# Retention stage of a two-block transformer kernel: values centred while they are turned, context states added in PSUM, hand-written order for each engine, and outputs passed on from SBUF

## What is computed

```python
def _ret_final_state(k, v, log_gamma):
    w = jnp.exp(log_gamma.astype(F32)[None, :] * jnp.arange(T - 1, -1, -1, dtype=F32)[:, None])
    return jnp.einsum('bthk,bthv->bhkv', k * w[None, :, :, None], v)
# per chunk, forwards and (flipped) backwards
    scores = jnp.einsum('bhik,bhjk->bhij', qc, kc) * d_intra
    o = jnp.einsum('bhij,bhjv->bhiv', scores, vc) + jnp.einsum('bhik,bhkv->bhiv', qc * q_decay, s)
    s = c_decay * s + jnp.einsum('bhjk,bhjv->bhkv', kc * k_decay, vc)
# in the token mixer
    o_r = _head_layernorm(o_rf + _flip(o_rb), ret_norm_w) * jax.nn.silu(rg)
    out = jnp.concatenate([o_g, o_r], axis=-1) @ w_out
```

## Time and profile before

| | |
|---|---|
| median of 3 runs | 3810.3 us (3804.82 to 3817.7) |
| the profiled execution | 3809.31 us, its span 3807.5 us |
| PE busy, share of the span | 3524.9 us, 93% |
| DVE, ACT, POOL busy | 2190.0, 1529.1, 734.2 us |
| last projection matmul of `in2` starts | 2691.4 us |
| retention stage on PE (to the first `out2` matmul) | 146.47 us, PE busy 89.59, DVE 91.30, ACT 58.35 |
| first output tile of `out2` done | about 2853 us |

### The profile page before, as it was taken

How to read it: one execution, slowest core, us unless ns; L and a number is a source line. 1 busy time by engine, 2 the same in 40 slices (tenths; PEclk the granted TensorE clock), 3 DMA queues, 4 the chain that set the end, 5 groups by cost and what they waited for, 6 DMA issues and landing times.

```text
span 3807.5 us, 45943 instructions
## 1 busy us (share of the span) xinstructions
PE 3524.9 (93%) x18417; PEld 2895.9 (76%) x18417; DVE 2190.0 (58%) x2898; ACT 1529.1 (40%) x1900; POOL 734.2 (19%) x334
## 2 busy tenths in 40 slices
PE   6999999999899899999998789999769699999996
PEld 4566677677687688888886567777547699999996
DVE  3343446545366555545325444545654899999996
ACT  3344442334222221121124433333342677777774
POOL 2111111122123222222223111111011222222210
PEclk9999999999999999999999999999889899999998
DMA  3111113143553144444311113132532899999996
GB/s 126 40 50 56 56 61 123 56 149 125 188 189 127 45 138 142 151 150 149 97 39 49 58 68 135 63 117 92 155 114 80 335 378 378 380 384 382 377 378 244
DMA packets 127268, 611.68 MB, mean 161 GB/s; under 512 B 14353, under 2 KB 15769, under 8 KB 102226
## 3 DMA queue, kind: packets, MB, share of 16 engines
q1 hardware_dynamic: 122306, 591.44, 42.4%
q0 software_dynamic: 4608, 16.78, 1.7%
q10 hardware_dynamic: 144, 0.52, 0.0%
HBM read 525.39 MB, written 83.27 MB: 160 GB/s over the span
## 4 chain that ended last, share of the span: by engine, by line
PE 81%; DVE 9%; ACT 4%; DMA 3%; issue 2%; POOL 1%; SPq 0%; DVEq 0%; ACTq 0%; POOLq 0%
PE bank L264 17%; PE bank L266 17%; PE bank L265 17%; PE bank L3085 4%; PE bank L3087 4%; PE bank L3086 4%; PE bank L3097 2%; PE bank L3095 2%; PE bank L3096 2%; PE bank L616 2%; PE bank L585 1%; PE bank L594 1%; PE bank L605 1%; DVE stg L1619 1%; DVE res L854 1%
## 5 line engine op out<-in xcount | busy, mean ns | idle before, releaser
L264 PE MATMUL bank<-XH,WH 128*128 128x512 f32 (+1 forms) x2696 | 1085.2, 403 | 97.1 <-DVE XL L2018 16.2
L266 PE MATMUL bank<-XH,WL 128*128 128x512 f32 (+1 forms) x2696 | 1055.4, 391 | 0.0
L265 PE MATMUL bank<-XL,WH 128*128 128x512 f32 (+1 forms) x2696 | 1053.5, 391 | 0.0
L252 POOL TENSOR_TENSOR WL<-WR,WH 128x1024 fp32r<-128x1024 f32 (+1 forms) x249 | 494.3, 1985 | 2161.1 <-ACT WH L244 2161.1
L264 PEld LDWEIGHTS bank<-XH,WH 128*128 128x128 f32 x2696 | 512.1, 190 | 267.0 <-issue 76.8
L265 PEld LDWEIGHTS bank<-XL,WH 128*128 128x128 f32 x2696 | 513.5, 190 | 108.8 <-issue 6.3
L266 PEld LDWEIGHTS bank<-XH,WL 128*128 128x128 f32 x2696 | 512.9, 190 | 105.7
L244 ACT ACTIVATE WH<-WR 128x1024 fp32r<-128x1024 f32 (+1 forms) x249 | 216.5, 870 | 612.6 <-PE bank L266 592.0
L3026 DVE TENSOR_TENSOR EL<-ER,EH 128x2816 fp32r<-128x2816 f32 x120 | 369.1, 3082 | 4.0 <-POOL warm L3269 4.0
L3021 ACT ACTIVATE EH<-ER 128x2816 fp32r<-128x2816 f32 x120 | 306.5, 2563 | 151.7 <-PE bank L3087 89.0
L3085 PE MATMUL bank<-EH,WH 128*128 128x352 f32 x1024 | 335.6, 328 | 1.5 <-DVE WL L3187 1.5
(11 more groups left out here) (511 smaller groups left out, 5009.0 us busy)
## 6 DMA issues: line engine op xcount, KB each, us to landing
ER<-in_wu_dram SPq DMA_DIRECT2D x48, 1408.0 KB, 9.1
ER<-in_wd_dram SPq DMA_DIRECT2D x40, 1408.0 KB, 9.6
aq<-in_w_ada_dram SPq DMA_DIRECT2D x96, 512.0 KB, 3.9
WR<-in_w_in_dram SPq DMA_DIRECT2D x89, 512.0 KB, 4.5
ER<-in_wg_dram SPq DMA_DIRECT2D x32, 1408.0 KB, 8.1
res<-in_wg_dram SPq DMA_DIRECT2D x16, 1408.0 KB, 8.5
res<-in_wu_dram SPq DMA_DIRECT2D x16, 1408.0 KB, 8.6
WR<-in_wg_dram SPq DMA_DIRECT2D x16, 1408.0 KB, 8.3
```

The costliest lines, as they stand in the source:

```text
L252: e.tensor_tensor(WL[:, n % 2 * 1024:n % 2 * 1024 + m], raw, hi.bitcast(F32), ALU.subtract).then_inc(*w_lo.up("w_lo", n))
L264: e.matmul(bank[bk][:, 0:b - a], whi, xhi, start=k == 0, stop=False)
L265: e.matmul(bank[bk][:, 0:b - a], whi, xlo, start=False, stop=False)
L266: mm = e.matmul(bank[bk][:, 0:b - a], wlo, xhi, start=False, stop=k == K - 1)
```

## The change

**Values.** The values are no longer turned by a transpose but by a product with a constant matrix, the identity minus 1/128 everywhere (`cn("mneg")`, made by DVE much earlier), which turns and centres them at once. The mean of the output is then zero, so `ret.msum` and `ret.mean` go. ACT squares straight from PSUM, then copies out.

**States.** The key copy of the further context chunk gets one chunk's decay more (`far`), and PE adds the two context chunks in PSUM. Each direction has eight products in two groups of four (`G8`), the second in bank 0 or 1. DVE's recurrence is one copy and seven multiply-adds per direction, written straight into the slots of `Ss`.

**Tables.** Masking and adding of `Dm` is done by POOL (`ret_pool_`), and its scale goes into DVE's multiplication of the scores.

**Order.** `ret_interleave` goes; the calls for each engine are written out. The rotations for head 1 are done inside the stage.

**Handing on.** `h2`, the landing place of the `D_o` tiles, lies over keys and values in `RM`. SP loads tiles 0 to 5 when head 3's scores are formed. Tiles 6 and 7 (heads 2 and 3) aren't stored; `out2` reads them where they are, in `aq`. The small transfers of router weights and `D_m5` come after the last `out2.lo`.

```diff
+    def ret_pe_(e):
+        e.wait_ge(*on("ret.cen"))
+        ret_v_pe(e, 0)
+        ret_k_pe(e, 0)
+        ret_scores_pe(e, 0)
+        ret_v_pe(e, 1)
+        ret_states_pe(e, 0)
+        ret_k_pe(e, 1)
+        ret_states_pe(e, 1)
+        ret_out_pe(e, 0)
+        ret_scores_pe(e, 1)
+        ret_root_pe(e, 0)
+        ret_k_pe(e, 2)
+        ret_v_pe(e, 2)
+        ret_out_pe(e, 1)
+        ret_states_pe(e, 2)
+        ret_scores_pe(e, 2)
+        ret_root_pe(e, 1)
+        ret_v_pe(e, 3)
+        ret_k_pe(e, 3)
+        ret_states_pe(e, 3)
+        ret_scores_pe(e, 3)
+        ret_out_pe(e, 2)
+        ret_root_pe(e, 2)
+        ret_out_pe(e, 3)
+        ret_root_pe(e, 3)
+
+    def ret_v_pe(e, h):
         e.wait_ge(*on("ret.v", h))
+        for c0, n in G10:
+            b = 6 + c0 // 4 % 2
+            e.wait_ge(*on.bank(b, "ret.vT", h, "N", c0))
+            for cc in range(c0, c0 + n):
+                mm = e.matmul(bank[b][:, (cc - c0) * 128:(cc - c0) * 128 + 128],
+                              rmem[h % 2]["v"][:, cc * 128:cc * 128 + 128], cn("mneg"), start=True, stop=True)
+            mm.then_inc(*ret_pe.up("ret.vT", h, "T", c0))
...
+    def ret_states_pe(e, h):
+        M = rmem[h % 2]
+        e.wait_ge(*on("ret.kT", h, "N", 8))
+        e.wait_ge(*on("ret.vT", h, "N", 8))
+        for n0, n in G8:
             for d in range(2):
+                b = d if n0 else 6 + d
+                e.wait_ge(*on.bank(b, "ret.S", h, d, n0))
                 for q in range(n0, n0 + n):
-                    cc = ORDERS[d][q]
...
+                    pair = ORDERS[d][0:2] if q == 0 else ORDERS[d][q + 1:q + 2]
+                    for i, cc in enumerate(pair):
+                        mm = e.matmul(bank[b][:, (q - n0) * 128:(q - n0) * 128 + 128],
+                                      M["keN"][d][:, cc * 128:cc * 128 + 128], M["vN"][:, cc * 128:cc * 128 + 128],
+                                      start=i == 0, stop=i == len(pair) - 1)
+                mm.then_inc(*ret_pe.up("ret.U", h, d, n0))
...
-        for k in range(2):
-            b = B_S[1][k]
-            e.wait_ge(*on("ret.ov", h, k))
-            e.wait_ge(*on.bank(b, "ret.mean", h, k))
-            e.matmul(bank[b][:, :], ones, M["o"][:, half(k)], start=True, stop=True).then_inc(*P.up("ret.msum", h, k))
...
+    def ret_out_act(e, h):
+        M = rmem[h % 2]
         for k in range(2):
             e.wait_ge(*on("ret.o", h, k))
+            e.activation(M["Ss"][1][:, half(k)], bank[B_S[1][k]][:, :], AF.Square).then_inc(*ret_act.up("ret.sq", h))
             if h > 1:
                 e.wait_ge(*on("o", 4 + h - 2))
...
+    def ret_pool_(e):
+        for h in range(4):
+            Dm = rmem[h % 2]["Dm"]
+            for d, mk in enumerate(("mle", "mge")):
+                e.wait_ge(*on("ret.dm", h, d))
+                e.tensor_tensor(Dm[:, d * 128:d * 128 + 128], Dm[:, d * 128:d * 128 + 128], cn(mk), ALU.mult).then_inc(
+                    *ret_pool.up())
+            e.wait_ge(*ret_pool.now)
+            e.tensor_tensor(Dm[:, 0:128], Dm[:, 0:128], Dm[:, 128:256], ALU.add).then_inc(*ret_pool.up("ret.mask", h))
...
+        ret_queries_dve(e, 0)
+        ret_scores_dve(e, 0)
+        ret_rope_dve(e, 1, "k")
+        ret_rope_dve(e, 1, "q")
+        ret_states_dve(e, 0)
+        ret_queries_dve(e, 1)
+        ret_scores_dve(e, 1)
+        ret_states_dve(e, 1)
+        ret_rope_dve(e, 2, "k")
+        ret_rope_dve(e, 2, "q")
+        ret_gate_dve(e, 0)
+        ret_norm_dve(e, 0)
+        ret_rope_dve(e, 3, "k")
+        ret_queries_dve(e, 2)
+        ret_scores_dve(e, 2)
+        ret_states_dve(e, 2)
+        ret_rope_dve(e, 3, "q")
+        ret_gate_dve(e, 1)
+        ret_norm_dve(e, 1)
+        ret_queries_dve(e, 3)
+        ret_scores_dve(e, 3)
+        ret_states_dve(e, 3)
+        ret_gate_dve(e, 2)
+        ret_norm_dve(e, 2)
+        ret_gate_dve(e, 3)
+        ret_norm_dve(e, 3)
...
+        e.wait_ge(*on("ret.sc", 3, 1))
+        for j in range(6):
+            e.wait_ge(*on("o", j))
+            e.dma_start(tj(h2, j), D_o[j]).then_inc(*d_fl[j].up("out2.o", j))
...
-        for s in d_o:
-            e.wait_ge(*s.end)
         for h in range(2):
             for j in range(8):
                 o = j * T + h * 512
-                e.wait_ge(*on("out2.o", h, j))
-                e.activation(XH3[:, o:o + 512], h2[:, o:o + 512], AF.Copy).then_inc(*A.up("out2.hi", h, j))
+                if j < 6:
+                    e.wait_ge(*on("out2.o", j))
+                e.activation(XH3[:, o:o + 512], out2_in(j)[:, half(h)], AF.Copy).then_inc(*A.up("out2.hi", h, j))
```

More of the change, by code:

```diff
@@ L2493, in ret_sp @@
         join(e, "in2")
[L2494 to L2502 removed]
+        ret_load_sp(e, 0, "g")
+        ret_load_sp(e, 1, "g")
+        for h in range(2):
             e.wait_ge(*on("ret.vT", h, "T", 8))
@@ L2581, in ret_act_ @@
     def ret_act_(e):
-        A = ret_act
         join(e, "gla")
         join(e, "in2")
-        ret_interleave([ret_head_act(e, h) for h in range(4)])
-    def ret_head_act(e, h):
-        A, M = ret_act, rmem[h % 2]
-        Dm = M["Dm"]
-        yield
+        ret_tables_act(e, 0)
+        ret_tables_act(e, 1)
+        turn_act(e, ret_act, rmem[0]["vN"], ("ret.vT", 0))
+        ret_k_act(e, 0)
+        turn_act(e, ret_act, rmem[1]["vN"], ("ret.vT", 1))
+        ret_k_act(e, 1)
+        ret_out_act(e, 0)
@@ L2606, in ret_head_act @@
             e.wait_ge(*on("ret.kT", h, "T", c0))
+            b = bank[6 + c0 // 4 % 2]
             for d in range(2):
-                e.activation(M["keN"][d][:, c0 * 128:(c0 + n) * 128], bank[6 + c0 // 4 % 2][:, 0:n * 128], AF.Identity,
-                             scale=lg[:, 16 + 4 * d + h:17 + 4 * d + h]).then_inc(*A.up("ret.kT", h, "N", c0))
-        yield
-        yield
-        yield
-        yield
-        yield
+                near, far = lg[:, 16 + 4 * d + h:17 + 4 * d + h], lg[:, 32 + 4 * d + h:33 + 4 * d + h]
+                if c0 < 8:
+                    e.activation(keN[d][:, c0 * 128:(c0 + n) * 128], b[:, 0:n * 128], AF.Identity, scale=near).then_inc(
+                        *ret_act.up("ret.kT", h, "N", c0))
+                else:
+                    for i in range(2):
+                        e.activation(keN[d][:, (8 + i) * 128:(9 + i) * 128], b[:, i * 128:i * 128 + 128], AF.Identity,
+                                     scale=far if i == d else near).then_inc(*ret_act.up("ret.kT", h, "N", c0))
@@ L2664, in ret_first_dve @@
             st.upto("ret.first", i)
-        for j, (h, x) in enumerate(((0, "k"), (1, "q"), (1, "k"))):
-            ret_rope_dve(e, h, x)
+        ret_rope_dve(e, 0, "k")
+        for j in range(3):
             st.upto("ret.first", 2 + j)
     def ret_dve_(e):
-        V = ret_dve
         join(e, "gla")
@@ L2723, in ret_head_dve @@
                                                ALU.add).then_inc(*V.up("ret.S", h, d, n0))
-                    prev[d] = dst
-        yield
-        yield
-        yield
-        yield
-        for k in range(2):
-            e.wait_ge(*on("ret.msum", h, k))
-            e.scalar_tensor_tensor(o_[:, half(k)], bank[B_S[1][k]][:, :], -1.0 / 128, o_[:, half(k)], ALU.mult,
-                                   ALU.add).then_inc(*V.up("ret.mean", h, k))
-        yield
-        yield
-        yield
+                    prev[d] = to
@@ L2781, in out2_sp @@
         join(e, "ret")
-        for s in d_o:
-            e.wait_ge(*s.end)
-        for h in range(2):
-            for j in range(8):
-                if h:
-                    e.wait_ge(*on("out2.o", 0, j))
-                e.dma_start(tj(h2, j)[:, half(h)], D_o[j][:, half(h)]).then_inc(*d_fl[j].up("out2.o", h, j))
         for j in range(8):
@@ L2815, in out2_pe @@
         e.wait_ge(*on("out2.m5c"))
-        e.wait_ge(*on.bank(0, "out2.m5"))
-        e.transpose(bank[0][0:8, 0:128], cf[:, 0:8], ident).then_inc(*P.up("out2.m5T"))
+        e.wait_ge(*on.bank(7, "out2.m5"))
+        e.transpose(bank[7][0:8, 0:128], cf[:, 0:8], ident).then_inc(*P.up("out2.m5T"))
         for m in range(8):
@@ L2906, in out2_dve @@
         join(e, "ret")
-        for s in d_o:
-            e.wait_ge(*s.end)
         e.scalar_tensor_tensor(cs_[:, 16:24], mod[:, 32:40, 0], 1.0, pr("norm2", 0, 8), ALU.add, ALU.mult).then_inc(*V.up())
         e.tensor_copy(cf[:, 0:8], mod[:, 40:48, 0]).then_inc(*V.up("out2.m5c"))
-        e.wait_ge(*on("out2.m5T"))
-        e.tensor_copy(ac2[0:8, 0:128], bank[0][0:8, 0:128]).then_inc(*V.up("out2.m5"))
         for h in range(2):
@@ L2915, in out2_dve @@
                 out2_lo(e, V, h, j)
+        e.wait_ge(*on("out2.lo", 1, 7))
+        e.wait_ge(*on("out2.m5T"))
+        e.tensor_copy(ac2[0:8, 0:128], bank[7][0:8, 0:128]).then_inc(*V.up("out2.m5"))
         w3 = wr_.rearrange("p (j e) -> p j e", e=16)
@@ L3297, in pe_program @@
         st.rest("in2", "end")
-        ret_interleave([ret_head_pe(e, h) for h in range(4)])
+        ret_pe_(e)
         out2_pe(e)
```

(1 more changed line is left out.)

195 lines of the change are left out of this document (84 added, 111 removed).

## The result

The changed kernel takes 3779.71 us, the median of 7 runs (3769.93 to 3792.79), against 3811.14 us for the kernel before in the same session (7 runs, 3804.82 to 3817.7): a ratio of 0.9917, 95% interval 0.9903 to 0.9931, so about 0.8% faster. The prediction was 3777, range 3763 to 3793. The profiled execution took 3782.39 us.

The account below looks back on a forecast made before the run. Hand-overs between engines were taken to bound the retention stage; 26.8 us less by head 3's end plus 6.0 at the hand-over made 32.8 less, from 3809.3 to 3776.5, said as 3777 us, range 3763 to 3793.

Parts of the forecast that it names:

- The sum: Whole kernel: 26.8 us less up to head 3's end plus 6.0 at the hand-over, 32.8 us less in all.
- What bounds the stage: Retention stage, 146.5 us: no engine is full, hand-overs between engines bound it, and savings should arrive whole at the end.
- States in PSUM: Heads' chunk products: DVE loses one step per direction, 0.8 us a head; PE's 28.0 us of waiting for the recurrence go.
- Centring: Heads' mean: 8.8 us of PE products and 5.3 of DVE subtractions go; turning values costs 1.1 us a head more.
- Tables to POOL: Masks of the heads: DVE loses 16 small operations, about 4.4 us; holding up between POOL and DVE costs 2.
- Written order: DVE's new list in the stage: 74.7 us of work, 32.0 of waits; head 3 ends at 2804, 26.8 us less.
- The walk: Stage's engine lists summed in order with old durations; the old lists came out 2.8 us late, which was taken off.
- Rival 2: Engine lists of the heads: late entries in fixed lists bring two more stalls of 8 us, kernel 3793 us; 14%.
- Handing on: Head 3's end to the first out2 tile: ACT starts sooner, out2.lo limits; 5.4 to 9.8 us less, 6.0 taken.
- The clock: PE in the stage: about a fifth of its work at 1.2 GHz, as the granted clock before was 0.80.
- rival 1: PE in the stage stays at the low clock: 12 to 13 us slower than before, kernel 3822 us; 3%.
- rival 4: PE in the stage does nearly no work at the low clock: kernel 3765 us; 13%.

Follow-up runs that it names:

- c4: The changed kernel with other lists for PE, ACT and DVE, found by a search with a walk over the lists: 3756.6 us, ratio 0.9866.
- c2: The kernel before with only the context states changed (added in PSUM, eight regions a direction, second four in banks 0 and 1): 3786.43 us, ratio 0.9944.
- a3: The changed kernel with PE's list altered, scores of heads 1 to 3 ahead of their chunk products: 3773.97 us, ratio 0.9914.
- a4: a3 with the context states of before, nine regions a direction in banks 6 and 7 only: 3785.93 us, ratio 0.9938.
- b3: The changed kernel with values turned by transposes again and the mean left out of the computation: 3778.42 us, ratio 0.9921.
- c1: The kernel before with the centring alone added, its order, states, masks and hand-over kept: 3804.19 us, ratio 0.9989.
- b1: The changed kernel with the mask products and their sum back on DVE, ahead of each head's scores: 3779.88 us, ratio 0.9922.
- a1: The changed kernel with its new operations called in the interleaved order of before: 3775.83 us, ratio 0.991.
- b4: The changed kernel with the old hand-over, heads 2 and 3 stored and half tiles loaded after all stores: 3786.06 us, ratio 0.9938.

## Why the prediction was right, step by step

**The sum.** It said 32.8 us less. The medians differ by 31.4, the profiled executions by 26.9 (3809.31 and 3782.39). In the profiles head 3 ends 23.8 us earlier instead of 26.8, the hand-over gives 6.6 instead of 6.0, and 3 us are lost behind the stage, which the sum had not. That the median of the changed kernel came within 3 us of 3777 is in part luck: its runs lie 22.9 us apart, and the profiled one is 5.4 us above it.

**What bounds the stage: right, with half of the gain in DVE's work.** Hand-overs bound it: with the same operations, c4 took another 20.7 us out of the stretch by order alone. But of the 24.4 us of the change itself DVE's own work gave 12.0 (88.0 to 76.0 us, the stretch less DVE's idle times in it) and its waits 12.4 (44.5 to 32.1). And what was saved arrived at the end but for 3 us.

**States in PSUM: the step that carries the result, and the prediction named its mechanism.** "PE's 28.0 us of waiting go" came true, and what it named as next, the turn that needs banks 6 and 7, is the 9.2 us of c2. Alone in the old order this part gives 22.8 us (c2), and taken back from a3's lists it costs 17.3 (a4).

**Centring.** A product turns at 1.8 times the cost of a transpose (12.8 against 7.1 us of PE for four heads), close to the factor of two taken from the earlier trace rows. By the Trainium skill's "4× faster for FP32" (TensorE: Matmul & The Clock Gate, Terms), 7.1 would have become 28.4, an estimate; the measurement decides against it. On the path the product costs 0.7 us (b3). Centring as a whole gave 4.9 us in the old order (c1).

**Tables to POOL: the sum had 4.4 of gain and 2 of cost; b1 has nothing.** The cost in longer DVE operations was about right (1.5 us), the gain was not, since the 3.1 us that go from DVE stood ahead of a wait (b1 leaves the scale, the rest of the 4.4, where the change put it). The prediction's estimate by the "exclusive lock" of the Trainium skill's SBUF — State Buffer (SBUF: two separate sides) was also that the move gives nothing. That agrees with b1, but not for its reason: the cost is 1.5 us for DVE's queries and not 4.8.

**Written order: the number held, its name didn't.** The walk put head 3's end at 2804, the trace has 2806.98; the waits of 11.2 and 6.7 us are 10.15 and 6.46, and the eleven idle times of DVE in the stretch add up to 32.1 us where the walk had 32.0. The rest, DVE's work, is 76 instead of 74.7 us (the terms given add to 74.6). PE's idle time ahead of head 2's keys, "some 10 us", is 8.6. But the prediction booked its 26.8 us under the written order and never priced the order by itself. The experiments give: operations 27.8 (a1), of them states 22.8 and centring 4.9, and the written order 3.4 the other way. A walk with the old order and the new operations would have told this: the one put on record after the result and before a1 ran ended near 2803 (measured 2803.84), against 2807 for the written order. The sum came near without this because its walk had the new operations in it; what was wrong is whose gain it was. Rival 2, another queue in order, is thus present in the result as the two waits for scores, which the sum had in it.

**Handing on: 6.0 predicted, 6.6 measured** in the profile; taken back in b4 it is 6.5. PE starts 1.66 us behind the last head (1.5 predicted). The low parts of `out2` take 13.7 us on DVE and POOL together (2807.81 to 2821.55) instead of 15.2.

**The clock.** 0.84 in the stage, near the 0.80 of before, so neither rival 1 nor rival 4. Whether products in place of transposes raise the clock stays open: in the stretch it is 0.83 in the changed kernel, b1 and b4 and 0.80 with transposes (b3), but 0.81 with the centring alone (c1) and 0.82 before.

## What to carry to other kernels

Before crediting a rewrite to its order, walk the old order with the new operations: here that one number separates them. A wait of the matmul engine for a bank that another engine reads piece by piece can be worth more than the instructions in it: one region less in the same two banks gave 12 us, where its instructions are 3 us. And when each engine's list is written by hand, put what the most loaded engine needs next first on the others: a few exchanged entries of PE's list gave 9 us (a3), a search over all lists 21 (c4). What a part is worth depends on the lists around it: the mean cost 4.9 us in one set and 21.2 in another.

## What the runs showed of the hardware

A POOL operation of 128 columns took 0.45 us when DVE was idle and mostly 1.3 to 1.43 beside a running DVE operation, while DVE's 1024 columns went from 1.22 to 1.47 us:

```profile
L2670 POOL TENSOR_TENSOR RM<-RM,con x8: 448/1334/1434, 2696.3 to 2776.7; 128x128 f32<-128x128 f32 x8
```

```profile
L2756 DVE TENSOR_TENSOR RM<-res,RM x8: 1217/1472/1475, 2698.7 to 2779.2; 128x1024 f32<-128x1024 f32 x8
```

(both from the changed kernel; shortest, median and longest in ns). The two look as if they took turns, one operation each, so the short one pays most: POOL 0.9 us, DVE 0.25. No run was made to show that. With operations of 512 columns, `out2`'s low parts, DVE took 0.69 us alone and 1.77 beside POOL, POOL 1.27 alone and 1.73:

```profile
2813.51 5.18 DVE L3033 TENSOR_TENSOR XL<-h,XH 128x512 fp32r<-128x512 f32 x3
2818.61 1.77 DVE L3033 TENSOR_TENSOR XL<-aq,XH 128x512 fp32r<-128x512 f32 x1
```

The second row starts three operations of DVE after the first, so DVE's starts lie 1.70 us apart: that is what a pair, one operation of each engine, took, where one after the other would be 1.96.
